# A recurrent turn with its input products split around the last level and one reciprocal placed later

## What is computed

```
def rwkv7_recurrence(r, decay, k, v, a, b):
    # S_t = S_{t-1} diag(decay_t) + (S_{t-1} a_t) b_t^T + v_t k_t^T ;  y_t = S_t r_t
    def step(state, inp):
        r_t, w_t, k_t, v_t, a_t, b_t = inp
        sa = jnp.einsum('bhvk,bhk->bhv', state, a_t)
        state = (state * w_t[:, :, None, :] + sa[..., None] * b_t[:, :, None, :]
                 + v_t[..., None] * k_t[:, :, None, :])
        y_t = jnp.einsum('bhvk,bhk->bhv', state, r_t)
        return state, y_t
...
y = rwkv7_recurrence(rh, dh, kh, vh, -kk, kk * ah)          # 32 heads of 64
mu = jnp.mean(y, axis=-1, keepdims=True)
var = jnp.mean(jnp.square(y - mu), axis=-1, keepdims=True)
y = ((y - mu) * lax.rsqrt(var + LNX_EPS)).reshape(B, S, D)
y = y * lnx_w + lnx_b + bonus
out = (y * g) @ w_o
```

## Time and profile before

| | us |
|---|---|
| median of 3 runs | 3323.56 |
| lowest and highest run | 3316.80, 3324.43 |
| the profiled execution | 3324.36 |
| its span in the profile | 3322.7 |
| the recurrence in it | 1016 to 1341 |

### The profile page before, as it was taken

The page is one execution under the profiler, slowest core; times in us unless marked ns, Lnnn a source line. Parts: engine busy times, 40 slices in busy tenths (PEclk is TensorE's granted clock), DMA queues, the critical chain, the costliest instruction groups (busy, mean ns, idle before and its releaser), DMA issues.

```text
span 3322.7 us, 65145 instructions
## 1 busy us (share of the span) xinstructions
PE 3198.1 (96%) x23206; PEld 2761.0 (83%) x23206; DVE 2284.9 (69%) x3387; ACT 1505.7 (45%) x2115; POOL 347.4 (10%) x526
## 2 busy tenths in 40 slices
PE   7999999989999999999999999999999999999998
PEld 6887777877887888888888888888778888888887
DVE  6657656578777886776666767776666766666675
ACT  5543443457645554444344434444444434444343
POOL 2001022000033442200000000200002000000002
PEclk9999999989999898999999999999999999999999
DMA  6654446446762110566666666677445666666664
GB/s 193 166 155 112 135 133 173 132 123 178 211 195 74 35 35 25 164 178 189 185 187 185 189 184 183 178 189 190 123 118 166 186 186 183 189 187 186 183 186 144
DMA packets 1001281, 524.25 MB, mean 158 GB/s; under 512 B 25750, under 2 KB 996396, under 8 KB 1000620
## 3 DMA queue, kind: packets, MB, share of 16 engines
q1 hardware_dynamic: 995756, 507.99, 54.2%
q0 software_dynamic: 4560, 13.05, 1.1%
q10 hardware_dynamic: 816, 1.11, 0.1%
HBM read 513.69 MB, written 8.39 MB: 157 GB/s over the span
## 4 chain that ended last, share of the span: by engine, by line
PE 82%; DVE 8%; issue 4%; ACT 4%; POOL 1%; DMA 0%; ACTq 0%; DVEq 0%; POOLq 0%; SPq 0%; PEldq 0%
PE proj L302 48%; PE proj L304 24%; DVE w_low L258 1%; ACT w_high L271 1%; DVE g L314 1%; DVE w_low L274 1%; PE side L2272 1%; PE side L828 1%; PE side L537 0%; PE side L2385 0%; PE side L2253 0%; PE side L536 0%; DVE g L2723 0%; DVE g L2719 0%; ACT w_high L252 0%
## 5 line engine op out<-in xcount | busy, mean ns | idle before, releaser
L302 PE MATMUL proj<-b_pair,w_high 128*128 128x512 f32 x3872 | 1384.6, 401 | 27.0 <-DVE g L314 9.9
L302 PE MATMUL proj<-a_pair,w_high 128*128 128x512 f32 x3664 | 1298.1, 399 | 40.5 <-DVE a_pair L1712 19.5
L274 DVE TENSOR_TENSOR w_low<-w_raw,w_high 128x1024 fp32r<-128x1024 f32 x688 | 838.4, 1225 | 407.2 <-ACT w_high L271 403.4
L304 PE MATMUL proj<-b_pair,w_low 128*128 128x256 f32 x3872 | 1091.2, 282 | 0.0
L304 PE MATMUL proj<-a_pair,w_low 128*128 128x256 f32 x3664 | 1031.0, 281 | 0.0
L271 ACT ACTIVATE w_high<-w_raw 128x1024 fp32r<-128x1024 f32 x696 | 732.5, 1058 | 532.1 <-PE proj L304 526.9
L302 PEld LDWEIGHTS proj<-b_pair,w_high 128*128 128x128 f32 x3872 | 733.8, 190 | 211.7 <-issue 17.9
L302 PEld LDWEIGHTS proj<-a_pair,w_high 128*128 128x128 f32 x3664 | 691.7, 189 | 209.1 <-issue 22.1
L304 PEld LDWEIGHTS proj<-b_pair,w_low 128*128 128x128 f32 x3872 | 738.8, 191 | 0.2
L304 PEld LDWEIGHTS proj<-a_pair,w_low 128*128 128x128 f32 x3664 | 696.9, 190 | 0.1
L258 DVE TENSOR_TENSOR w_low<-w_raw,w_high 128x1024 fp32r<-128x1024 f32 x276 | 348.2, 1269 | 245.7 <-ACT w_high L252 240.2
(11 more groups left out here) (572 smaller groups left out, 2706.8 us busy)
## 6 DMA issues: line engine op xcount, KB each, us to landing
w_raw<-in_mlp_w_up_dram SPq DMA_DIRECT2D x256, 512.0 KB, 4.3
w_raw<-in_mlp_w_down_dram SPq DMA_DIRECT2D x256, 512.0 KB, 3.9
w_raw<-in_w_in_dram SPq DMA_DIRECT2D x112, 512.0 KB, 3.8
w_raw<-in_rwkv_w_rkv_dram SPq DMA_DIRECT2D x96, 512.0 KB, 4.2
w_raw<-in_w_kvf_dram SPq DMA_DIRECT2D x64, 512.0 KB, 4.1
w_raw<-in_w_out_dram SPq DMA_DIRECT2D x32, 512.0 KB, 3.9
w_raw<-in_rwkv_w_o_dram SPq DMA_DIRECT2D x32, 512.0 KB, 4.0
w_raw<-in_fox_w_q_dram SPq DMA_DIRECT2D x32, 512.0 KB, 4.0
```

What stands on the lines that cost most here:

```text
L274: eng.tensor_tensor(wl[slot][:], raw[slot][:], wh[slot][:].bitcast(F32), ALU.subtract)\
L302: pe.matmul(ps[bank][:, :].rearrange("p (a n) -> p a n", a=2), wh[slot][:, k, :], pair[:, :, kk, :], start=kk == 0, stop=False)
L304: mm = pe.matmul(ps[bank][:, 0:S], wl[slot][:, k, :], pair[:, 0, kk, :], start=False, stop=kk == KT - 1)
```

## The change

On TensorE `inputs` takes the halves that it is to do. In level 5 only half 0 is done before L2433, and half 1 after it. `joint` runs the systems of half 0 of the next turn after the wait for `U` of half 0, and waits for `U` of half 1 behind them. On VectorE both systems of the next turn follow the inverse of half 0, and the inverse of half 1 stands behind `read(j)`.

```
-            def inputs(i):
-                for s in range(2):
+            def inputs(i, only):
+                for s in only:
...
             def joint(i):
                 par = i % 2
-                for s in range(2):
-                    pe.wait_ge(sem("rw_u"), u_done(i, s, 5))
+                pe.wait_ge(sem("rw_u"), u_done(i, 0, 5))
                 if i < LAST:
                     systems(i + 1, 0)
+                pe.wait_ge(sem("rw_u"), u_done(i, 1, 5))
...
                     elif lv == 5:
-                        inputs(i)
+                        inputs(i, (0,))
...
+                inputs(i, (1,))
                 joint(i)
...
-                kf = []
-                for s in range(2):
-                    if i:
-                        kf.append(inverse(fin, s))
-                    if i < LAST:
+                kf = [inverse(fin, 0)] if i else []
+                if i < LAST:
+                    for s in range(2):
                         systems(j, s)
...
                 if i < LAST:
                     read(j)
                 if i:
+                    kf.append(inverse(fin, 1))
                     gated(fin, scaled(fin, kf))
```

## The result

| | before | changed |
|---|---|---|
| median | 3319.25 us (6 runs) | 3300.48 us (6 runs) |
| lowest to highest | 3314.41 to 3324.43 | 3288.03 to 3309.34 |
| the profiled execution | 3324.36 | 3308.54 |

The ratio is 0.9938, with a 95% interval of 0.9918 to 0.9958: by the medians the change gains 18.8 us (13.9 to 27.2 by the interval). The direction was right, the size too small. One part of the distance is the base: the forecast started from 3323.56, the median of three runs of the kernel before, and over all six runs that median is 3319.25, 4.3 us lower.

What follows compares the result with a forecast made beforehand. TensorE, busy 96% of the span, bounds the kernel, so only its idle time and clock count. Terms 0.5 + 0.3 + 6.9 + 2.6 = 10.3 us, some 15 with three such turns; 12 taken: 3312 us, range 3302 to 3323.

Steps and rivals of the forecast that it cites:

- TensorE's order: End of a turn: split input products and relaxed wait for U gain 0 in turns 0 to 6, 0.5 us in turn 7.
- Idle time before L2346: Before the product with the new state: the later second reciprocal removes 3.8 us of TensorE idle time in turns 2, 5, 6.
- No fall behind L2346 without the second idle stretch: Turns 5 and 6: if the 1.85 us wait made the clock fall, it now stays up; turn 5 gains 5.2 us by clock.
- the second idle stretch: TensorE's wait before L2346, the product with the new state; 1.85 us in turn 5.
- rival A: Around L2346: only the wait goes, the clock falls anyway for narrow matmuls; gain 4.3 us, 3319 to 3320 us; chance 0.22.
- Length of such a turn: A turn with the clock up, bound by VectorE's keys, then the sigmoids and L2272, takes 36.8 us; turn 5 took 43.72.
- X: The start of the systems L2253 for half 0 on TensorE, which opens the work of the next turn.
- Behind the last X, 3.1 us: End of the recurrence: 2.6 us for turn 6, bounded by VectorE's wait in turn 7, and 0.5 us in turn 7.
- In turns 1 to 4 the clock falls at X and they cost 39.5 on the mean, and the change leaves them alone: Turns 1 to 4 of the recurrence: low clock from about X on, 39.5 us on the mean, untouched by the change.
- Rival B: TensorE meets VectorE's keys and the sigmoids instead, loses 1.7 us there and the clock falls; 3322 to 3324 us; chance 0.10.
- Rival C: Before L2253: input products there keep the clock up in turns 1 to 4, 11 us more, 3301 us; chance 0.08.
- Rival D: Low-clock turns: VectorE's later reciprocal delays keys, sigmoids and L2272 by up to 1.71 us; uncovered, 3334 us; chance 0.05.

Runs made afterwards that it cites:

- the kernel with filled products: Kernel before, with the products L2335 and L2336 issued three times in turns 1 to 6, the wait before L2346 kept; 0.9978 of before.
- `bt` first: Changed kernel, with GpSimd computing product bt of half 0 (L2005) before L2000 of half 1; 0.9965 of before.
- the kernel with no idle time at X: Changed kernel with GpSimd's L2005 of half 0 before L2000 of half 1, and VectorE's bonus products behind the level 5 copies and decayed; 0.9928 of before.

## Where the prediction was right, and which step failed

- **TensorE's order, 0 us, and 0.5 in turn 7:** right as far as it can be measured. The edit alone gives 1.0005, and the wait in turn 7 is gone. One reading was a little off: TensorE did not end as early as before but 0.14 us later, so 0.81 us of idle time stayed and not 0.95.
- **Idle time before L2346, 3.8 us:** right in kind and size: 4.1 us in the first profile and 6.4 in the second of before, 0 to 0.8 in the three of the changed kernel. What stays in a turn at the high clock is 0.25 us, where 0.14 was read.
- **No fall behind L2346 without the second idle stretch:** right, against rival A. The changed kernel runs turns of 36.83 us at 1.00, the kernel with filled products turns of 37.9.
- **Length of such a turn, 36.8 us, set by VectorE's `keys` and the sigmoids:** the length is right to 0.1 us, and with no idle time at X it stays. That the sigmoids set it alone is not shown, since the squares end with them.
- **Behind the last X, 3.1 us:** right in size, in part by luck. From X of turn 6 to the matmul of the next projection that waits for the outputs of turn 7 the profiles of before took 59.2 and 57.0 us, those of the changed kernel 56.5, 55.2 and 52.9: 58.1 and 54.9 on the mean, 3.2 apart. Executions of one kernel differ there by 2.2 and 3.6 us, as much as the term itself.
- **"In turns 1 to 4 the clock falls at X and they cost 39.5 on the mean, and the change leaves them alone":** this step failed. It put what happens at X at nothing, and that brought 4.8 us. Its reasons were that nothing is waited for before L2346 in these turns, and that work and idle time ahead of X have the same sum. Neither says how often a turn meets a fall at X, or how long the clock is then low, once the turns ahead of it are shorter. Over the two profiles of before and the three of the changed kernel, turns 1 to 5:

| | before (10 stretches) | changed (15 stretches) |
|---|---|---|
| fall at X | 7, mean 39.5 us | 8, mean 38.6 us |
| past X at the high clock | 3, mean 42.3 us | 7, mean 36.6 us |
| sum of five, mean | 201.7 us | 188.3 us |

The five stretches gain 13.3 us. For them the forecast had 9: its 12 less the 2.6 of turn 6 and the 0.5 of turn 7. Had only the price of a turn past X changed, from 42.3 to 36.6 in 3 of 10, it would be 5 x 0.3 x 5.7 = 8.5 us. So that term was sized well. The other 4.8 us were missed, about half in each of two ways. Turns fall at X less often, 8 in 15 and not 7 in 10, and each one that does not fall is 2.9 us shorter: 5 x 0.17 x 2.9 = 2.4 us. And those that do fall come back sooner, 38.6 and not 39.5: 5 x 0.53 x 0.9 = 2.4 us. I had read the kinds of turn as fixed and only their price as changed.

The second way can be followed in the rows. A turn of 37.5 us tends to be followed by its like: in the profiles of the changed kernel, of VectorE's edit alone and of `bt` first, that was so in eight of ten cases, and the other two were followed by 39.0. The kernel before had no turn of 37.5 in its two profiles; its shortest was 37.92, with 0.35 us of idle time before L2346, and 40.88 came behind it. So it seems that the length of a turn decides where the next one meets the clock. That is argued, and no run tested it.

Whether turns fall less often because of the change or by chance, ten and fifteen stretches do not settle, the less so since they come from two and three executions and hang together within each. Also open is why the clock held past X in all five stretches of the kernel with the second idle time filled, with the same 0.95 us of idle time there. In the kernel before seven of ten stretches had a fall at X, so a part of what that kernel gains is not explained by work put before L2346.

The recurrence then accounts on the mean of the profiles for 13.3 + 3.2 = 16.5 us, against 18.8, 18.3 and 20.8 by the medians of the three series in which both kernels ran. The rest lies within the interval. It is also no more than what the code that both share varies by: from the same matmul of the next projection to the end the two profiles of before took 1981.6 and 1977.4 us, those of the changed kernel 1981.6, 1982.2 and 1983.6.

That the time lay below the range has a second reason beside the 4.8 us. The median of before came out at 3319.25 and not at 3323.56, 4.3 us lower, by the spread of that kernel alone. The gain of 18.8 us, taken from 3323.56, would have given 3304.8, inside the range.

- **Rival B**, the second idle stretch only moved: it did not happen. Before L2385, the first product of a level, TensorE waits for VectorE 2.7, 3.3 and 2.7 us in the three profiles of the changed kernel, 2.7 in both of before.
- **Rival C**, 3301 us because the first fall goes too: the time hits this number, but not by its mechanism. C laid it to the input products ahead of the first idle stretch, and with TensorE's edit alone the clock fell at X in all of turns 1 to 5. The changed kernel still falls there in 8 of 15.
- **Rival D**, a delay where the clock is low: it happens, at no cost. In turn 3 of the changed kernel VectorE stands idle for 0.37 us until TensorE is through with the systems of half 1, and the turn is shorter than before.

## What to carry to other kernels

In a loop of serial turns, look at the granted clock of each turn before pricing a wait: here a turn in which the clock fell was 0.7 to 4 us longer than the 36.83 us of one at the high clock where it fell at X, and 2.4 to 5.3 us longer, beside the 1.6 us of idle time, where it fell behind the second idle stretch. Where two short jobs of another engine are both due, the one for which TensorE waits goes first, even if the other would fit in neatly; this one move was the whole of the gain that could be measured. And a wait that is relaxed brings nothing while another releaser is 0.04 us behind it: follow each operand of the waiting instruction back before counting on it.

## What the runs showed of the hardware

Work that changes nothing can pay for itself. The 1.7 us of repeated products in each of six turns made the kernel before faster by 0.2% (0.03 to 0.41%), and with them the granted clock stood at 1.00 (2.4 GHz) in turns where it had been at 0.50 (1.2 GHz) for up to 13 us.

The fall is not a fixed answer to an idle time of a given length: 1.5 us were followed by it in four turns and not in a fifth, and 0.95 us in seven of ten stretches of the kernel before. It also came without an idle stretch over 0.12 us, in two turns of the kernel with no idle time at X, behind short matmuls that kept TensorE busy for 3.28 of 3.40 us.

The turns that fall at X take 37.5 to 38.0, 39.0 or 40.3 to 41.2 us in most cases, whichever kernel it is. What makes executions of one kernel differ by 20 us is open: the clock in the turns is a part of it, but the code behind the recurrence, which is the same in all kernels, took between 1975.6 and 1988.3 us over the profiles as well.
